# Hybrid decoder step: value product on four column groups of the array, and the normed input's split held resident and in HBM

## The chip, the cores and the metric

One core of one Trainium2 chip runs the whole step in one launch. The metric is the time of an execution on the device, in microseconds (us), lower is better. Engines are named as the profile names them: PE is TensorE (PEld its weight loads), DVE is VectorE, ACT is ScalarE, POOL is GpSimd, SP is SyncE, which here only issues DMAs.

## The reference

One layer for one prompt of 2048 tokens and eight decode rows with 4096 cached tokens each, d_model 1024, all in f32. The two edits touch the combined projection and, for the decode rows, the product of softmax weights with the cached values.

```
h = rms_norm(x, norm_g)
z = h @ w_in              # (1024 x 4096): ret q,k,v,gate | diff q,k,v,gate
# 4 retention heads: chunks of 128 tokens with a carried state, rms norm, times silu(gate)
# 4 differential heads: two softmax maps of 64 dims, a = p0 - lam * p1, o = a @ v
# decode rows: the same, with keys and values gathered by page_table from cache_k, cache_v
y = x + concat(o_ret * silu(gate), o_diff * silu(gate)) @ w_out
```

A f32 product of z is made of three products of rounded parts (fp32r): high h with high w, high h with low w, low h with high w, where low = value - high.

## The kernel before

Five stages follow each other, each a block in which every engine runs its own program and semaphores order them.

Stage 1, `setup_stage` (to 123.7 us), norms 17 tiles (one of the decode rows, 16 of 128 prompt rows). For each n ACT squares x (L323), POOL makes the inverse root, DVE normalises (L380), PE turns the tile with eight transposes (L473) into two banks, and ACT and DVE each copy one half into the resident g.hT (`keep_a` L332, `keep_b` L390). Meanwhile PE projects the decode rows with w_in in eight column groups of 2 MB. SP issues, in its order, `load_w(n)` (L266, two buffers, waits for the product of group n-2), `load_x(2n+1)` and `load_x(2n+2)` (L261, three buffers), n from 1 to 7, then the eight chunks of the first head's weights (L306), which ACT and DVE split (L350, L457).

Stage 2, `retention_stage`, runs four heads in a loop; stage 3, `diff_stage`, four more. A head begins with its projection: for each of 16 tiles, PE does 24 matmuls (`project_tile`, L563 to L565) on the halves h_hi and h_lo, which ACT (`split_h_high`, L541) and DVE (`split_h_low`, L549) make from g.hT again in each head, three slots ahead. ACT takes the result out of the bank (`keep_z`, L581 on); rotation and gate follow on DVE and POOL, and in stage 3 also a norm of queries and keys: DVE's sums of squares, POOL's inverse root, DVE's scaling (L1368) and rotary steps, and the parts of the keys (L1380).

Beside each head one decode row is worked. During the projection its 16 pairs of key pages come through a ring of four slots; DVE multiplies each with the query (L620) and sums (L626). After a softmax over the pages (`row_softmax_dve`, `row_softmax_pe`, `row_softmax_act`), 16 pairs of value pages come through the same ring, and PE multiplies each page (128 tokens x 512) with its scores (128 x 8) into s.row_bank (`row_values`, L691), a pair as two matmuls on 8 of the 128 columns of the array. Each f32 matmul stands as two records in the trace. The pairs are placed among PE's other work by `pairs_at`: in stage 2, one pair in each of the chunks t=3 to 12 and two in t=13 to 15; in stage 3, one in each of the attention units i=2 to 15, and two in 6 and 7.

A chunk of stage 2 is, on PE: turn of the next query and key (L1031, L1032), values, inner product (L1038), outputs (L1058, L1059) and the state's increment (L1061); ACT and DVE copy and mask between these, and in t=5 to 12 also split the next head's weights (L523, L529). The stages 4 and 5 (the decode rows' end and the output projection) do not use what is changed.

Of the kernel before, what the change touches and what calls it, by code (L numbers as in the profile page):

```python
# [21 lines left out]
F32 = mybir.dt.float32  # L22
# [24 lines left out]


# [5 lines left out]
def shape_constants():  # L54
# [29 lines left out]
    own_head = np.zeros((HC, NH, P), f)  # L84
    for i in range(HC):
        own_head[i, i // 2] = 1.0
    pick_map = np.zeros((HC, P), f)
    for i in range(HC):
        pick_map[i, i % 2] = 1.0
    own_row = np.zeros((NS, NS, P), f)  # L90
    for i in range(NS):
# [8 lines left out]
        "c_own_head": own_head.reshape(HC, NH * P),  # L100
# [90 lines left out]
def setup_stage(nc, io, g):  # L191
    with ExitStack() as ctx:
        sb = lambda n, s, d=F32: ctx.enter_context(nc.sbuf_tensor(n, s, d))
        sem = lambda n: ctx.enter_context(nc.semaphore(n))
# [15 lines left out]
        hsT = sb("hsT", [P, DC, NS])  # L210
        zs = sb("z_sample", [NS, 4 * D])
# [20 lines left out]
        kept_b = sem("s1_kept_b")  # L232
        z_ready = sem("s1_z_ready")
# [23 lines left out]
        def _(sp):  # L257
# [57 lines left out]
            sp.wait_ge(stored, 48)  # L315

        @block.scalar
        def _(act):
# [7 lines left out]
            def keep_a(n):  # L326
                act.wait_ge(turned, n + 1)
                src_ = bank[n % 2][:].rearrange("p (c r) -> p c r", c=4)
                if n == 0:
                    nc.scalar.copy(hsT[:, 0:4, :], src_[:, :, 0:NS]).then_inc(kept_a, 1)  # L330
                else:
                    nc.scalar.copy(g.hT[:, 0:4, (n - 1) * P:n * P], src_).then_inc(kept_a, 1)  # L332
# [38 lines left out]
        def _(dve):  # L371
# [12 lines left out]
            def keep_b(n):  # L384
                dve.wait_ge(turned, n + 1)
                src_ = bank[2 + n % 2][:].rearrange("p (c r) -> p c r", c=4)
                if n == 0:
                    dve.tensor_copy(hsT[:, 4:8, :], src_[:, :, 0:NS]).then_inc(kept_b, 1)
                else:
                    dve.tensor_copy(g.hT[:, 4:8, (n - 1) * P:n * P], src_).then_inc(kept_b, 1)  # L390
# [71 lines left out]
        def _(pe):  # L462
# [16 lines left out]
            pe.wait_ge(kept_b, 1)  # L479
            for n in range(8):  # L480
# [8 lines left out]
                turn(2 * n + 2)  # L489

# [17 lines left out]
HALVES = 2 * NT  # L508

# [22 lines left out]
def half_of_h(g, n):  # L532
    t, half = n // 2, n % 2
    return g.hT[:, 4 * half:4 * half + 4, t * P:(t + 1) * P]


def split_h_high(act, s, g, it, n):

    if n >= s.HSLOTS:
        act.wait_ge(s.half_used, it * HALVES + n - s.HSLOTS + 1)  # L540
    act.copy(s.h_hi[n % s.HSLOTS][:], half_of_h(g, n)).then_inc(s.half_high, 1)  # L541


def split_h_low(dve, s, g, it, n):

    dve.wait_ge(s.half_high, it * HALVES + n + 1)
    if n >= s.HSLOTS:
        dve.wait_ge(s.half_used, it * HALVES + n - s.HSLOTS + 1)
    dve.tensor_tensor(s.h_lo[n % s.HSLOTS][:], half_of_h(g, n), s.h_hi[n % s.HSLOTS][:],  # L549
                      ALU.subtract).then_inc(s.half_low, 1)  # L550


def project_tile(pe, s, g, it, t):
# [3 lines left out]
    for half in range(2):  # L557
        n = 2 * t + half
        pe.wait_ge(s.half_low, it * HALVES + n + 1)
        hi, lo = s.h_hi[n % s.HSLOTS], s.h_lo[n % s.HSLOTS]  # L560
        for c in range(4):
            wc = 4 * half + c
            pe.matmul(s.z_bank[t % 2][:], hi[:, c, :], g.w_hi[:, wc, :], start=(wc == 0), stop=False)  # L563
            pe.matmul(s.z_bank[t % 2][:], hi[:, c, :], g.w_lo[:, wc, :], start=False, stop=False)  # L564
            last = pe.matmul(s.z_bank[t % 2][:], lo[:, c, :], g.w_hi[:, wc, :], start=False, stop=(wc == DC - 1))  # L565
        last.then_inc(s.half_used, 1)


def keep_z(act, s, g, it, t):
# [9 lines left out]
    act.wait_ge(s.half_used, it * HALVES + 2 * t + 2)  # L579
# [55 lines left out]
def row_softmax_dve(dve, s, g, it, step):  # L635
    sc = s.scores[:].rearrange("p g s -> p s g")
# [9 lines left out]
    elif step == 2:  # L646
        dve.wait_ge(s.row_pe, q + 2)
        dve.tensor_tensor(s.scores[:], s.scores[:], bc(s.row_bank[:, 0:HC].unsqueeze(1), [P, NPAGE, HC]),
# [7 lines left out]
    elif step == 5:  # L656
        dve.wait_ge(s.values_used, it * NPAIR + NPAIR + VALUES_CREDIT)
        dve.tensor_tensor(s.row_own[:], s.row_bank[0:HC, :], g.own_head[:], ALU.mult).then_inc(s.row_dve, 1)
# [5 lines left out]
def row_softmax_pe(pe, s, g, it, step):  # L664
# [10 lines left out]
    elif step == 3:  # L675
        pe.wait_ge(s.row_dve, d + 7)
        pe.matmul(s.row_bank[:], g.pick_map[:], s.row_own[:], start=True, stop=True).then_inc(s.row_pe, 1)


def row_softmax_act(act, s, it):  # L680
    act.wait_ge(s.row_dve, it * ROW_DVE + 4)
    act.activation(s.scores[:], s.scores[:], ACT.Exp, scale=QSCALE).then_inc(s.row_exp, 1)


def row_values(pe, s, it, j):

    if j == 0:
        pe.wait_ge(s.row_dve, it * ROW_DVE + 6)
    pe.wait_ge(s.ring_loaded[(NPAIR + j) % RING], ring_at(it, NPAIR + j))
    for i in range(2):  # L690
        last = pe.matmul(s.row_bank[0:HC, :], s.scores[:, 2 * j + i, :], s.ring[(NPAIR + j) % RING][:, i, :],  # L691
                         start=(j == 0 and i == 0), stop=(j == NPAIR - 1 and i == 1))
    last.then_inc(s.values_used, 1)
# [55 lines left out]
def shared_tensors(nc, ctx, s):  # L749
# [7 lines left out]
    s.scores = sb("scores", [P, NPAGE, HC])  # L757
# [3 lines left out]
    s.row_own = sb("row_own", [HC, 512])  # L761
# [11 lines left out]
    s.half_high = sem("half_high")  # L773
# [1242 lines left out]
```

## Time and profile before

| | |
|---|---|
| median of 3 runs | 2217.17 us (2214.16 to 2220.43) |
| profiled execution | 2217.28 us, span 2215.6 us |
| mean granted TensorE clock | 0.914 |
| stage 1, to the first projection matmul | 123.7 us |
| stage 2, four heads | 123.7 to 778.0 us |
| stage 3, four heads | 778.0 us to the start of stage 4 |
| stage 5, output projection | 1943 to 2215.6 us |
| DMA over the span | 237.36 MB, mean 107 GB/s |

The profile is one execution. An engine's busy share is a mean over stages that have different limits, so it is read stage by stage. In a timeline row the first number is the start in us, the second the time, and what stands in brackets is how long the engine had been idle and what ended that.

### The profile page before, as it was taken

The page shows a single profiled execution, that of the slowest core. Times are in us where ns is not written, and L with a number is a line of the kernel's source. Part 1 is how long each engine was busy: PE and PEld are TensorE (multiplying, and loading weights), DVE is VectorE, ACT ScalarE, POOL GpSimd, SP SyncE. Part 2 cuts the span into 40 slices and gives each one's busy share as a digit, 9 for nine tenths or more (in the row PEclk, how much of TensorE's full clock was granted, in tenths as well). Part 3 has the DMA queues.
Part 4 walks back from the last instruction along what each step waited for, and adds up shares of the span by engine and source line. Part 5 has one row for each costly group of instructions (what it writes and reads, how often), then busy time and mean ns, then how long its engine had stood idle before and what let it go on. Part 6 is the DMA issues. An engine that isn't in the chain of part 4 may idle for free. (4 is left out here: it accounts for less than half of the span.)

```text
span 2215.6 us, 34308 instructions
## 1 busy us (share of the span) xinstructions
PE 1841.8 (83%) x8316; PEld 1261.9 (57%) x8316; DVE 1361.4 (61%) x2561; ACT 811.1 (37%) x2203; POOL 591.8 (27%) x1500
## 2 busy tenths in 40 slices
PE   6778998998998798589885898858989579657998
PEld 2267476476486376356763566634666446416887
DVE  2569468478477368577586675876757767462121
ACT  2333332332332233356343564435644346410000
POOL 4612322322422424121342112421214311240000
PEclk9989899998998899699996999979999789858999
DMA  7633533532622532321132311323212241053441
GB/s 288 230 120 97 175 106 100 173 104 90 195 91 89 158 110 77 104 97 59 52 94 90 102 63 45 96 81 115 63 36 91 60 150 44 11 155 129 136 141 69
DMA packets 164068, 237.36 MB, mean 107 GB/s; under 512 B 14963, under 2 KB 77060, under 8 KB 163732
## 3 DMA queue, kind: packets, MB, share of 16 engines
q1 hardware_dynamic: 157828, 218.22, 31.5%
q0 software_dynamic: 6048, 17.11, 2.1%
q8 instruction: 55, 0.90, 0.2%
q14 instruction: 137, 1.12, 0.2%
HBM read 207.00 MB, written 28.28 MB: 106 GB/s over the span
## 5 line engine op out<-in xcount | busy, mean ns | idle before, releaser
L563 PE MATMUL s_z<-g_w_hi,s_h_hi 128*128 128x512 f32 x1024 | 416.8, 407 | 63.0 <-DVE s_h_lo L549 63.0
L564 PE MATMUL s_z<-g_w_lo,s_h_hi 128*128 128x512 f32 x1024 | 411.3, 402 | 0.0
L565 PE MATMUL s_z<-g_w_hi,s_h_lo 128*128 128x512 f32 x1024 | 410.7, 401 | 0.0
L541 ACT CAST s_h_hi<-g_hT 128x512 fp32r<-128x512 f32 x256 | 157.4, 621 | 480.0 <-PE s_z L565 455.1
L549 DVE TENSOR_TENSOR s_h_lo<-g_hT,s_h_hi 128x512 fp32r<-128x512 f32 x256 | 181.5, 714 | 150.1 <-ACT s_h_hi L541 114.7
L563 PEld LDWEIGHTS s_z<-g_w_hi,s_h_hi 128*128 128x128 f32 x1024 | 196.5, 192 | 123.6 <-DVE s_h_lo L549 77.8
L691 PE MATMUL s_row<-s_ring,s_scores 128*8 128x512 f32 x512 | 246.5, 610 | 1.4 <-DVE s_row_stat L655 1.3
L1290 ACT ACTIVATE s_weights<-s_sc,s_neg_max 128x512 f32<-128x512 f32 (+3 forms) x320 | 196.3, 625 | 75.3 <-DVE s_neg_max L1433 53.1
L565 PEld LDWEIGHTS s_z<-g_w_hi,s_h_lo 128*128 128x128 f32 x1024 | 196.4, 192 | 47.9
L564 PEld LDWEIGHTS s_z<-g_w_lo,s_h_hi 128*128 128x128 f32 x1024 | 196.9, 192 | 45.5
L1550 PE MATMUL s_o<-s_vg,s_aT 128*128 128x128 f32 x1088 | 152.0, 287 | 52.5 <-ACT s_aT L1272 48.9
L1428 DVE TENSOR_REDUCE s_chunk_min<-s_sc 128x1 f32<-128x512 f32 (+3 forms) x288 | 161.9, 616 | 49.7 <-PE s_sc L1537 49.5
L1550 PEld LDWEIGHTS s_o<-s_vg,s_aT 128*128 128x128 f32 x1088 | 130.9, 192 | 74.5 <-ACT s_aT L1272 73.4
L620 DVE TENSOR_TENSOR s_ring<-s_ring,s_q_row 128x1024 f32<-128x1024 f32 x128 | 159.4, 1246 | 1.9 <-DVE s_qk L962 0.6
L626 DVE TENSOR_REDUCE s_scores<-s_ring 128x16 f32<-128x1024 f32 x128 | 156.2, 1220 | 4.4
L733 POOL TENSOR_TENSOR s_fin_x<-s_o_ms,s_rsum 128x4 f32<-128x4 f32 x16 | 3.1, 194 | 522.2 <-DVE s_vg L719 522.2
L1536 PE MATMUL s_sc<-s_kT,s_qT 128*128 128x512 f32 (+3 forms) x320 | 134.9, 422 | 5.7 <-ACT s_kT L1240 3.0
L1537 PE MATMUL s_sc<-s_kT,s_qT 128*128 128x512 f32 (+3 forms) x320 | 117.6, 378 | 0.0
L1871 DVE TENSOR_TENSOR s_y<-s_y_bank,s_x_in 128x512 f32<-128x512 f32 (+1 forms) x34 | 21.9, 685 | 155.0 <-PE s_y_bank L1913 155.0
L1272 ACT COPY s_aT<-s_z 128x512 f32<-128x512 f32 (+3 forms) x160 | 81.6, 524 | 74.3 <-PE s_z L1522 72.9
L1452 DVE SCALAR_TENSOR_TENSOR s_weights<-s_weights,s_coef,s_weights 128x512 f32<-128x512 f32 (+3 forms) x160 | 101.8, 685 | 10.7 <-DVE s_coef L1445 10.7
L1911 PE MATMUL s_y_bank<-g_wo_hi,s_u_hi 128*128 128x512 f32 x272 | 108.0, 397 | 0.0
(228 smaller groups left out, 3062.1 us busy)
## 6 DMA issues: line engine op xcount, KB each, us to landing
s_ring<-in_cache_k SPq DMA_DIRECT2D x256, 256.0 KB, 2.7
s_ring<-in_cache_v SPq DMA_DIRECT2D x256, 256.0 KB, 2.8
w_raw<-in_w_in SPq DMA_DIRECT2D x8, 2048.0 KB, 8.4
s_w_raw<-in_w_in SPq DMA_DIRECT2D x64, 256.0 KB, 3.4
s_u_in<-u_scratch SPq DMA_DIRECT2D x17, 512.0 KB, 4.0
x_in<-in_x_prompt SPq DMA_DIRECT2D x16, 512.0 KB, 5.6
u_scratch<-s_u_out POOLq DMA_DIRECT2D x64, 128.0 KB, 2.5
s_x_in<-in_x_prompt SPq DMA_DIRECT2D x16, 512.0 KB, 4.0
```

Source lines behind the costliest of these rows:

```text
L541: act.copy(s.h_hi[n % s.HSLOTS][:], half_of_h(g, n)).then_inc(s.half_high, 1)
L549: dve.tensor_tensor(s.h_lo[n % s.HSLOTS][:], half_of_h(g, n), s.h_hi[n % s.HSLOTS][:], ALU.subtract).then_inc(s.half_low, 1)
L563: pe.matmul(s.z_bank[t % 2][:], hi[:, c, :], g.w_hi[:, wc, :], start=(wc == 0), stop=False)
L564: pe.matmul(s.z_bank[t % 2][:], hi[:, c, :], g.w_lo[:, wc, :], start=False, stop=False)
L565: last = pe.matmul(s.z_bank[t % 2][:], lo[:, c, :], g.w_hi[:, wc, :], start=False, stop=(wc == DC - 1))
L620: dve.tensor_tensor(slot[:], slot[:], bc(s.q_row[:].unsqueeze(1), [P, 2, 512]), ALU.mult).then_inc(s.keys_times_q, 1)
L626: dve.tensor_reduce(s.scores[:, 2 * j:2 * j + 2, :], s.ring[j % RING][:].rearrange("p i (s f) -> p i s f", f=DH), AX, ALU.add).then_inc(s. ...
L691: last = pe.matmul(s.row_bank[0:HC, :], s.scores[:, 2 * j + i, :], s.ring[(NPAIR + j) % RING][:, i, :], start=(j == 0 and i == 0), stop=(j ...
L1290: act.activation(dst, score_bank[e % 4][:, 0:w], ACT.Exp, bias=neg_max[i % 2][:, m:m + 1], scale=-1.0, accum_out=sums[i % 2][:, m, j:j + 1 ...
L1428: chain.step(dve.tensor_reduce(chunk_min[:, j:j + 1], score_bank[e % 4][:, 0:w], AX, ALU.min))
L1536: pe.matmul(b[:, 0:w], qT[i % 2][:, m, :], keys, start=True, stop=False)
L1550: last = pe.matmul(banks["o"][:, 0:P], aT[k % 2][:, x * P:(x + 1) * P], s.vg[:, kb, 0:P], start=(kb == 0), stop=(kb == i))
```

## The change

First, the split of the normed input is made once. In stage 1 ACT's `keep_a` copies both halves of a tile into the resident g.h_hi (rounded to fp32r; it takes the place of g.hT), and DVE's `keep_b` subtracts that from the bank into one of four buffers, from which SP stores it (`store_low`, two DMAs of 256 KB a tile) to a scratch in HBM. In the heads the two split functions are gone; PE takes the high part from g.h_hi, and SP reads the low part back in 32 DMAs of 256 KB per head through four slots (`load_low`), in its order ahead of key pages. The loop of page loads in SP is unrolled by tile for that. Stage 3's slots lie on memory that the attention uses, so SP waits for a new semaphore, weights_free, at a head's start. Stage 1's semaphores are cleared and a barrier follows, so that there are enough for what comes.

Second, `row_values` takes two pairs (a quad of pages) with four matmuls, each on its own group of 32 columns of the array and its own 32 partitions of row_bank, where they add up apart; the matmul that picks the heads (L677) sums them. The stationary operand is 32 columns wide: the 8 scores of the page and those of the next three, whose products are not used. The quads stand in stage 2 at chunks 4, 6, 8, 10 and 12 to 15, in stage 3 at units 3, 5, 7, 9, 11 and 13 to 15.

```diff
 def setup_stage(nc, io, g):
...
+            def store_low(t):
+                sp.wait_ge(kept_b, t + 2)
+                for half in range(2):
+                    sp.dma_start(io["h_low"][t, :, 512 * half:512 * half + 512],
+                                 low[2 * (t % 2) + half][:].rearrange("p c x -> p (c x)").bitcast(F32)).then_inc(low_stored[t % 2], 16)
+
             for n in range(1, 8):
                 load_w(n)
                 load_x(2 * n + 1)
                 load_x(2 * n + 2)
+                store_low(2 * n - 2)
+                store_low(2 * n - 1)
+            store_low(NT - 2)
+            store_low(NT - 1)
...
             def keep_a(n):
                 act.wait_ge(turned, n + 1)
...
+                for half in range(2):
+                    src_ = bank[2 * half + n % 2][:].rearrange("p (c r) -> p c r", c=4)
...
+                        last = nc.scalar.copy(g.h_hi[:, 4 * half:4 * half + 4, (n - 1) * P:n * P], src_)
+                last.then_inc(kept_a, 1)
...
             def keep_b(n):
-                dve.wait_ge(turned, n + 1)
...
+                dve.wait_ge(kept_a, n + 1)
...
+                t = n - 1
+                if t >= 2:
+                    dve.wait_ge(low_stored[t % 2], 32 * (t // 2))
+                for half in range(2):
...
+                    last = dve.tensor_tensor(low[2 * (t % 2) + half][:], src_,
+                                             g.h_hi[:, 4 * half:4 * half + 4, t * P:(t + 1) * P], ALU.subtract)
+                last.then_inc(kept_b, 1)
...
+    nc.clear_and_free_semaphores(used)
+    nc.all_engine_barrier()
...
+def load_low(sp, io, s, g, it, n):
+
+    k = it * HALVES + n
+    slot = n % LOWSLOTS
+    sp.wait_ge(g.low_used, k + 1)
     t, half = n // 2, n % 2
...
+    sp.dma_start(s.low[slot][:].rearrange("p c x -> p (c x)").bitcast(F32), io["h_low"][t, :, 512 * half:512 * half + 512]
+                 ).then_inc(g.low_loaded[slot], 16)
...
 def project_tile(pe, s, g, it, t):
...
-        pe.wait_ge(s.half_low, it * HALVES + n + 1)
-        hi, lo = s.h_hi[n % s.HSLOTS], s.h_lo[n % s.HSLOTS]
+        pe.wait_ge(g.low_loaded[n % LOWSLOTS], (s.first_head + it) * (16 * HALVES // LOWSLOTS) + 16 * (n // LOWSLOTS + 1))
         for c in range(4):
             wc = 4 * half + c
...
+            hi, lo = g.h_hi[:, wc, t * P:(t + 1) * P], s.low[n % LOWSLOTS][:, c, :]
...
+        last.then_inc(g.low_used, 1)
...
+def row_values(pe, s, it, jj):
+
+
+    if jj == 0:
         pe.wait_ge(s.row_dve, it * ROW_DVE + 6)
...
+    for j in (2 * jj, 2 * jj + 1):
+        pe.wait_ge(s.ring_loaded[(NPAIR + j) % RING], ring_at(it, NPAIR + j))
+    for q in range(COLS):
+        j, i = 2 * jj + q // 2, q % 2
+        last = pe.matmul(s.row_bank[QUAD * q:QUAD * (q + 1), :], s.scores_all[:, 2 * j + i:2 * j + i + QUAD // HC, :].rearrange("p g s -> p (g s)"),
+                         s.ring[(NPAIR + j) % RING][:, i, :], start=(jj == 0), stop=(jj == NPAIR // 2 - 1),
+                         tile_position=(0, QUAD * q))
+    last.then_inc(s.values_used, 2)
...
 def retention_stage(nc, io, g):
...
-        pairs_at = {t: ([t - 3] if t < 13 else [2 * t - 16, 2 * t - 15]) for t in range(3, NT)}
+        quads_at = {4: [0], 6: [1], 8: [2], 10: [3], 12: [4], 13: [5], 14: [6], 15: [7]}
...
+                for n in range(LOWSLOTS):
+                    load_low(sp, io, s, g, it, n)
                 load_sample_q(sp, io, s, it, it)
-                for j in range(NPAIR):
+                for j in range(RING):
                     load_pages(sp, io, s, g, it, it, j)
+                for t in range(NT):
+                    for n in (2 * t + LOWSLOTS, 2 * t + LOWSLOTS + 1):
+                        if n < HALVES:
+                            load_low(sp, io, s, g, it, n)
+                    if t + RING < NPAIR:
+                        load_pages(sp, io, s, g, it, it, t + RING)
...
 def diff_stage(nc, io, g):
...
+        quads_at = {3: [0], 5: [1], 7: [2], 9: [3], 11: [4], 13: [5], 14: [6], 15: [7]}
...
+                sp.wait_ge(weights_free, it + 1)
+                for n in range(LOWSLOTS):
+                    load_low(sp, io, s, g, it + NH, n)
...
+                act.sem_inc(weights_free, 1)
```

## Rows read from the trace of the kernel before

**Rows 1.** Section 1 of the page: busy us, share of the span, instructions of each engine.
```profile
PE 1841.8 (83%) x8316; PEld 1261.9 (57%) x8316; DVE 1361.4 (61%) x2561; ACT 811.1 (37%) x2203; POOL 591.8 (27%) x1500
```

**Rows 2.** Groups of instructions of the page (busy, mean ns; idle before, releaser).
```profile
...
L549 DVE TENSOR_TENSOR s_h_lo<-g_hT,s_h_hi 128x512 fp32r<-128x512 f32 x256 | 181.5, 714 | 150.1 <-ACT s_h_hi L541 114.7
...
L691 PE MATMUL s_row<-s_ring,s_scores 128*8 128x512 f32 x512 | 246.5, 610 | 1.4 <-DVE s_row_stat L655 1.3
```

**Rows 3.** Windows (us; busy and count of PE, PEld, DVE, ACT, POOL): two projections.
```profile
123.70:215.80 92.10, 92.10 (x384) 73.78 (x384) 75.10 (x95) 28.95 (x74) 19.44 (x21) 0.97 0.33 102
...
778.00:884.40 106.40, 97.02 (x404) 75.11 (x404) 78.34 (x126) 40.25 (x99) 36.09 (x96) 0.97 0.31 97
```

**Rows 4.** Timeline of stage 1 (start us, us, engine, line): DVE, ACT, SP.
```profile
34.47 1.28 DVE L380 SCALAR_TENSOR_TENSOR h_nat<-x_in,rstd,norm_g_rows 128x1024 f32<-128x1024 f32 x1 [8.47 <-POOLq L363]
...
70.67 1.05 ACT L323 ACTIVATE junk<-x_in 128x1024 f32<-128x1024 f32 x1
...
74.91 1.28 DVE L380 SCALAR_TENSOR_TENSOR h_nat<-x_in,rstd,norm_g_rows 128x1024 f32<-128x1024 f32 x1 [1.45 <-issue]
...
86.61 0.38 SPq L266 DMA_DIRECT2D w_raw<-in_w_in  x1
...
110.94 4.91 DVE L457 TENSOR_TENSOR g_w_lo<-w_raw,g_w_hi 128x512 fp32r<-128x512 f32 x8 [0.44 <-ACT g_w_hi L350]
```

**Rows 5.** DMA issues of the page: KB each, median us from issue to landing.
```profile
s_ring<-in_cache_k SPq DMA_DIRECT2D x256, 256.0 KB, 2.7
...
w_raw<-in_w_in SPq DMA_DIRECT2D x8, 2048.0 KB, 8.4
```

**Rows 6.** Timeline between a stage 2 projection and its chunks: DVE, PE.
```profile
377.31 1.50 DVE L620 TENSOR_TENSOR s_ring<-s_ring,s_q_row 128x1024 f32<-128x1024 f32 x1 [0.16 <-DVE s_qk L962]
...
382.60 0.47 PE L1031 MATMUL s_turn<-g_ident,s_qk 128*128 128x128 f32 x1 [6.67 <-DVEq L963]
```

**Rows 7.** Timeline of the chunks of stage 2, second head: PE and ACT.
```profile
390.27 0.42 PE L1031 MATMUL s_turn<-g_ident,s_qk 128*128 128x128 f32 x1
...
393.65 0.42 PE L1031 MATMUL s_turn<-g_ident,s_qk 128*128 128x128 f32 x1
...
403.63 0.28 ACT L712 ACTIVATE s_junk<-s_o 128x128 f32<-128x128 f32 x1 [2.01 <-PE s_o L1059]
...
403.89 0.61 ACT L523 CAST g_w_hi<-s_w_raw 128x512 fp32r<-128x512 f32 x1
...
403.96 1.88 PE L691 MATMUL s_row<-s_ring,s_scores 128*8 128x512 f32 x4
...
407.08 1.88 PE L691 MATMUL s_row<-s_ring,s_scores 128*8 128x512 f32 x4
...
435.26 3.60 PE L691 MATMUL s_row<-s_ring,s_scores 128*8 128x512 f32 x8
...
443.52 0.79 PE L563 MATMUL s_z<-g_w_hi,s_h_hi 128*128 128x512 f32 x1 [1.37 <-DVE s_h_lo L549]
```

**Rows 8.** Timeline of DVE in a stage 3 projection.
```profile
1130.04 0.42 DVE L1357 SCALAR_TENSOR_TENSOR s_vg<-s_th,s_vg 128x256 f32<-128x256 f32 x1
...
1137.17 0.69 DVE L1368 TENSOR_TENSOR s_zqk<-s_zqk,s_rq 128x512 f32<-128x512 f32 x1 [1.81 <-POOLq L1333]
...
1140.51 0.69 DVE L549 TENSOR_TENSOR s_h_lo<-g_hT,s_h_hi 128x512 fp32r<-128x512 f32 x1 [0.30 <-PE s_z L565]
...
1144.11 0.42 DVE L1357 SCALAR_TENSOR_TENSOR s_vg<-s_th,s_vg 128x256 f32<-128x256 f32 x1
```

**Rows 9.** Timeline at the start of a stage 3 head: PE.
```profile
1067.40 0.80 PE L563 MATMUL s_z<-g_w_hi,s_h_hi 128*128 128x512 f32 x1 [4.08 <-DVE s_h_lo L549]
```

**Rows 10.** Timeline of attention units of stage 3: PE (units 6, 7), DVE (late unit).
```profile
948.75 3.60 PE L691 MATMUL s_row<-s_ring,s_scores 128*8 128x512 f32 x8
...
958.51 3.60 PE L691 MATMUL s_row<-s_ring,s_scores 128*8 128x512 f32 x8
...
1038.62 2.48 DVE L1428 TENSOR_REDUCE s_chunk_min<-s_sc 128x1 f32<-128x512 f32 x4 [2.36 <-PE s_sc L1537]
```

More of the change, by code:

```diff
@@ L210, in setup_stage @@
         hsT = sb("hsT", [P, DC, NS])
+        low = [sb(f"low{i}", [P, 4, P], F32R) for i in range(4)]
         zs = sb("z_sample", [NS, 4 * D])
@@ L232, in setup_stage @@
         kept_b = sem("s1_kept_b")
+        low_stored = [sem(f"s1_low_stored{i}") for i in range(2)]
         z_ready = sem("s1_z_ready")
@@ L315, in _ @@
             sp.wait_ge(stored, 48)
+            for i in range(2):
+                sp.wait_ge(low_stored[i], 32 * (NT // 2))
         @block.scalar
@@ L676, in row_softmax_pe @@
         pe.wait_ge(s.row_dve, d + 7)
-        pe.matmul(s.row_bank[:], g.pick_map[:], s.row_own[:], start=True, stop=True).then_inc(s.row_pe, 1)
+        pe.matmul(s.row_bank[0:2, :], g.pick_map[:], s.row_own[:], start=True, stop=True).then_inc(s.row_pe, 1)
 def row_softmax_act(act, s, it):
     act.wait_ge(s.row_dve, it * ROW_DVE + 4)
-    act.activation(s.scores[:], s.scores[:], ACT.Exp, scale=QSCALE).then_inc(s.row_exp, 1)
-def row_values(pe, s, it, j):
-    if j == 0:
+    act.activation(s.scores, s.scores, ACT.Exp, scale=QSCALE).then_inc(s.row_exp, 1)
+def row_values(pe, s, it, jj):
+    if jj == 0:
         pe.wait_ge(s.row_dve, it * ROW_DVE + 6)
[L689 to L693, printed above, removed]
+    for j in (2 * jj, 2 * jj + 1):
+        pe.wait_ge(s.ring_loaded[(NPAIR + j) % RING], ring_at(it, NPAIR + j))
+    for q in range(COLS):
+        j, i = 2 * jj + q // 2, q % 2
[3 more added lines that the diff above has]
+    last.then_inc(s.values_used, 2)
 def row_store(pool, io, s, it, row):
@@ L1176, in diff_stage @@
         av_done = sem("av_done")
+        weights_free = sem("weights_free")
         block = ctx.enter_context(nc.Block())
-        pairs_at, left = {}, list(range(NPAIR))
-        for i in range(2, NT):
-            pairs_at[i] = [left.pop(0) for _ in range(2 if i in (6, 7) else 1)]
-        assert not left
+        quads_at = {3: [0], 5: [1], 7: [2], 9: [3], 11: [4], 13: [5], 14: [6], 15: [7]}
         NB = NT // 2
@@ L1971, in build @@
             hb = lambda n, sh, d=F32: heads.enter_context(nc.sbuf_tensor(f"g_{n}", sh, d))
-            g.hT = hb("hT", [P, DC, SEQ])
+            g.h_hi = hb("h_hi", [P, DC, SEQ], F32R)
+            g.low_loaded = [heads.enter_context(nc.semaphore(f"g_low_loaded{i}")) for i in range(LOWSLOTS)]
+            g.low_used = heads.enter_context(nc.semaphore("g_low_used"))
             g.w_hi = hb("w_hi", [P, DC, 512], F32R)
```

138 lines of the change are left out of this document (55 added, 83 removed).

## The prediction

> **What bounds the kernel now.** I read the busy table first: PE is busy 83% of the span, with no other engine near it [rows 1]. That share hides four kinds of stretch, so the windows come next. The reader is to see there that a stage 2 projection keeps PE busy all of its 92.1 us, with 384 matmuls, while a stage 3 projection takes 106.4 us of which PE is busy 97.0 and DVE 78.3 [rows 3]. So PE ends the first and something else paces the second. The groups tell what the two edits touch: the low split L549 is 181.5 us of DVE, with an idle time of which 114.7 us ended by ACT's high split, and the value product L691 is 246.5 us of PE [rows 2]. The timelines then say, stage by stage, what arrives last. Stage 1 is a chain of weight loads, squares, norms and copies [rows 4, 5]. In a chunk of stage 2 that has one value pair, PE follows itself from value to value, 3.12 us apart (403.96 to 407.08) [rows 7]. Between projection and chunks PE waits 6.67 us for DVE's rotation [rows 6]. In a stage 3 projection DVE repeats every 14.07 us (1130.04 to 1144.11) [rows 8]. Stages 4 and 5 are not touched.
>
> **Stage 1 gets longer.** The split itself is cheap: per tile ACT copies two halves instead of one, and DVE subtracts two instead of copying one. What costs is the place of the stores. SP issues in order, so load_w(n+1) now stands behind store_low(2n-1), which waits for keep_b(2n), which DVE runs after normalise(2n+1), whose x was queued behind load_w(n). Before, x was the only thing that held SP, and weight loads ran ahead. The new cycle: the 2 MB load lands in 8.4 us [rows 5]; x, a quarter of that size, 2.1 behind it (estimate); square to normalise 4.24 (70.67 to 74.91) [rows 4]; normalise 1.28; two subtracts at the 0.714 us of L549 [rows 2], 1.43; two issues at 0.38 [rows 4], 0.76. Sum 18.2 us. The first cycle is read directly, since its normalise began at 34.47: 34.47 + 1.28 + 1.43 + 0.76 = 37.9 for the second weight group, and five cycles more make 128.9 for the last, which was issued at 86.61 [rows 4]: +42.3. Its tail was 110.94 + 4.91 - 86.61 = 29.2 [rows 4]. Now it is a cycle of 18.2, the last tile's 4.24 + 1.43, and only then the first head's weights, which used to be fetched earlier: issue 0.38, landing 2.7 by the 256 KB row [rows 5], a cast of 0.6, the eight splits 4.91: 32.5, +3.3. Clearing the semaphores and the second barrier is in no row; it lies between nothing and the 7.8 us that pass between the end of the splits at 115.85 and the first matmul of stage 2 at 123.70 [rows 3], and I take 3. Together **+49**; 38 if x lands beside its weights (five times 2.1 less), 60 if the stores slow each cycle by 2. SP, ACT, DVE and PE all wait in this cycle, so nothing covers it.
>
> **Stage 2.** The projections stay: PE had no wait in them [rows 3], so taking 32 splits a head from ACT and DVE frees nothing there. The 32 low loads a head, 256 KB each, land in some 2.7 us [rows 5] and are prefetched four deep; two loads a tile against 5.75 us (92.1 / 16). I cost them at nothing; without that cover each tile would pay up to 2.7 us. Then the tail. DVE did the last keys after the last tile, a product of 1.50 us at 377.31 and then a sum, and PE's wait of 6.67 us ended behind them [rows 6]. Without 32 splits it does them before that tile is ready; the rotation starts some 2.7 us earlier and POOL's sine products, which ran beside the keys, become the last: I estimate 3 us saved (bounds 1.5 and 4.2), **-12** over four heads. The next head's first matmul waited 1.37 us for a split (443.52) [rows 7]; its low part is already there: **-4**.
>
> The value product: four records (two matmuls) take 1.88 us, eight take 3.60 [rows 7], so one record costs 0.43. A quad has eight. No row shows two of them sharing the array, so the price is bounded by 8 x 0.43 = 3.44 (no overlap) and 2 x 0.43 = 0.86 (all four groups together). The two records of a matmul use the same column group and the order of issue is kept, so only the second record of one and the first of the next can run together: five steps of eight, **2.15 us**. I take that, since it is the middle and follows from the order of the records. A chunk with a quad then costs PE 3.12 - 1.71 + 2.15 = 3.56 less what overlaps at its ends, some 3.3; a chunk without one can't fall to PE's 1.4, for it then goes with ACT: square 0.28 at 403.63, weight cast 0.61 at 403.89, turned copy, inner, mask [rows 7], about 2.4. The chunks from t=3 on, now from 393.65 to 435.26 + 3.60 + 0.9 = 439.8 [rows 7], 46.1 us, become 3.4 (t=3, still at half clock, as 390.27 to 393.65 [rows 7]) + 4.6 + 4 x 2.4 + 7 x 3.25 = 40.3. The clock is the open point: it is low in the chunks without values until the first value product comes (the chunk before is 3.38 us long), and four such chunks now stand between the quads. If they ran at that length again it would be +4. I take the middle, -4 a head, **-16**.
>
> **Stage 3.** Of the four splits in each DVE cycle of 14.07 us, two lie inside the wait for POOL's norm that ends at 1137.17 (1.81 us of it left) and two outside, 0.9 and 0.6 us (from 1140.51, and before 1144.11) [rows 8]. Without them the cycle is 12.5, still over PE's 11.5 (48 matmuls at 92.1 / 384 [rows 3]). Seven cycles give -11.3, the three splits ahead of the first tile another 2.1 and their waits 0.9: -14.3 a head, **-57**. Bound: 11 if page loads, which now stand before low loads in SP's order, hold a tile back. At the head's start PE waited 4.08 us to 1067.40 [rows 9]; low loads go when ACT leaves its last unit, 2.7 to landing [rows 5]: -2 for three heads, **-6**, and the change of stage gives nothing. The new wait for weights_free holds SP, and behind it the queries and pages, but no longer than that.
>
> In the attention units values are hidden as long as DVE and ACT pace: two units with two pairs each lie 9.76 us apart (948.75 to 958.51) [rows 10], as others with one do. Late units have DVE waiting 2.36 us for scores (1038.62) [rows 10], so there PE counts. Quads at 9, 11, 13, 14, 15 cost 2.15 - 1.71 = 0.44 more each, the pairs gone from 8, 10 and 12 give about 0.4 each: **+4**.
>
> Sum: 49 - 12 - 4 - 16 - 57 - 6 + 4 = -42. The profiled execution took 2217.28 us (median 2217.17, so no correction): **2175 us**.
>
> A page rule bears on the value product. The trace shows each further value record costing its full 0.43 us, four of them 1.88 and eight 3.60 [rows 7]. The Trainium skill, "TensorE: Matmul & The Clock Gate" (Part 3, Packing small matmuls), states that matmuls on other column groups run nearly together, 2.38 times as fast for three of them, in strict order. By 2.38 a quad would be 3.44 / 2.38 = 1.45 us, between my middle and the full overlap, and the time about 2150, nearest to A. "TensorEngine Tiling (Array Packing)" (Key Properties) states against the change that switching the tiling mode drains the engine; a switch stands before and after each quad here, and by that rule a quad gains less. No run here shows either.
>
> **The rivals.**
> A, full overlap: quads of about 0.95. Quad chunks fall to the 2.4 of ACT's chain; SP's page loads then limit the last four. Against the middle -4 a head in stage 2 and -4 in stage 3: 2175 - 16 - 17 = **2142**. For: the groups are independent. Against: two records per matmul in order.
> C, no overlap, ends slower: 3.44 a quad. In stage 2 a quad chunk takes 3.12 + 1.73 = 4.85, some 4.6 on the average with the last one shorter, and the chunks between cannot use the time they were given, being paced by ACT: 3.4 + 6 + 4 x 2.4 + 7 x 4.6 = 51.2, +5 a head and with the clock some +6.5, +26 instead of -16. In stage 3 1.73 more on five late units less hidden parts, +6 a head, +24 instead of +4. 2175 + 42 + 20 = **2237**. It decides from a quad of about 2.9 us on that stage 1 outweighs the rest.
> D, the stores do not lengthen stage 1, because loads already run far enough ahead: 2175 - 46 = **2129**. Against: the SP order is plain.
> E, the change does not do what it says in stage 3: low loads stuck behind page loads in SP's order, projections remain at 105: 2175 + 57 = **2232**. Against: DVE sums a page some two tiles before the low part behind it is needed.
>
> **How the numbers follow.** B (the forecast) 0.38, A 0.23, C 0.26, D 0.06, E 0.07. About 0.3%, 6.7 us, is what a measurement can tell from no change. B holds 2148 to 2205 by its bounds (-11 and +11 in stage 1, 3 a head of values either way). Faster: B 0.35, A 0.23, D 0.06 = 0.64; same: 0.03 of B, 0.03 of C and E = 0.06; slower 0.30. The range reaches to A and C with stage 1 at its bounds: **2128 to 2250**.
>
> **What would show it.** Stage 1: the SP rows of load_w spaced 18 us, and the first projection at about 172 instead of 123.70. Values: start to start of the quad's eight records, 0.43 (C), five steps (B), or nearly together (A), and the spacing of quad and plain chunks, with the granted clock beside them. Stage 2: PE's idle before L1031, 3.6 instead of 6.67. Stage 3: DVE's cycle 12.5, and no PE wait on a low load. It would be wrong first of all if the quad's records or the setup cycle have another length.

## The result, and the profile after

The changed kernel takes 2156.03 us (median of 4 runs, 2151.84 to 2158.10), the kernel before 2218.80 in the same sets of runs (2214.16 to 2226.56). The ratio is 0.9711, with a 95% interval of 0.9679 to 0.9744: faster by 2.9%, 62.8 us, where 42 were forecast. The profiled execution took 2157.04 us.

The busy table of the changed kernel, to set against [rows 1]: PE does as many instructions as before and is busy 115 us less.

```profile
span 2155.4 us, 33493 instructions
## 1 busy us (share of the span) xinstructions
PE 1726.8 (80%) x8316; PEld 1271.0 (59%) x8316; DVE 1200.6 (56%) x2322; ACT 675.1 (31%) x1964; POOL 568.3 (26%) x1500
```

To see where the time went, each trace is cut at the same events of PE: the first and last matmul of each projection, the first turn (stage 2) or first score (stage 3) behind it, the last state increment or the closing product of a head, and the next head's first matmul. The table gives the difference from the profiled execution of before, in us, summed over four heads. The experiments are told further down; they stand here so that they can be compared.

| kernel | stage 1 | st. 2 projection | wait to chunks | chunks | tails, starts | st. 3 projection | wait to units | units | starts, stage 4 | sum |
|---|---|---|---|---|---|---|---|---|---|---|
| changed | +51.3 | -3.7 | -9.2 | -12.8 | -1.7 | -43.1 | -20.2 | -18.7 | -1.6 | -60.2 |
| values only | +4.6 | -4.3 | +0.1 | -22.4 | -0.3 | -1.2 | +0.2 | -15.9 | -1.6 | -41.4 |
| low part only | +54.7 | -3.4 | -9.2 | -6.0 | -2.4 | -42.1 | -23.5 | +9.6 | -0.4 | -22.6 |
| one group | +53.9 | -9.3 | -9.2 | +13.3 | -2.7 | -43.3 | -20.9 | +47.3 | -2.9 | +25.6 |
| weights ahead of stores | +25.5 | -7.2 | -9.2 | -10.4 | -1.0 | -45.3 | -20.0 | -18.4 | -0.3 | -86.3 |
| four raw buffers | +48.5 | -2.7 | -9.2 | -22.5 | -1.8 | -43.9 | -19.3 | -14.7 | +2.0 | -63.8 |
| unread matmuls, st. 2 | +49.7 | -3.0 | -9.0 | -34.0 | -1.9 | -46.8 | -19.7 | -16.7 | +2.7 | -78.7 |
| all three | +24.4 | -4.9 | -9.0 | -35.1 | -1.0 | -47.0 | -20.9 | -17.5 | -1.0 | -112.9 |

Stage 5, which stands in no column, differs by less than 1 us. Each row is one execution. Where the code of a column is the same, executions differ by up to 6 us in stage 1 (48.5 to 54.7) and up to 4 in the units (-14.7 to -18.7). So stage 1 cost 51 us, stage 3 gave 84, and stage 2 gave 27.

**Stage 1.** SP's timeline of the changed kernel: load_w is L269, load_x is L264, the stores are L305. A row joins the four stores of two tiles; the second pair waits, within the row, for the next tile's subtract.

```profile
92.03 0.45 SPq L269 DMA_DIRECT2D w_raw<-in_w_in  x1
92.52 1.23 SPq L264 DMA_DIRECT2D x_in<-in_x_prompt  x2
106.11 3.19 SPq L305 DMA_DIRECT2D h_low_scratch<-low  x4
109.34 0.46 SPq L269 DMA_DIRECT2D w_raw<-in_w_in  x1
...
123.32 3.19 SPq L305 DMA_DIRECT2D h_low_scratch<-low  x4
126.56 0.44 SPq L269 DMA_DIRECT2D w_raw<-in_w_in  x1
```

The reader is to see that each weight load follows its stores at once and that nothing is issued between 93.75 and 106.11: SP stands at the wait in store_low. The cycle is 17.3 us (92.03 to 109.34), where it was 18.2 in the forecast, and the last weights are issued at 126.56; before, they ran ahead, the last at 86.61 [rows 4].

**The value product.** PE's timeline in chunks of the second head, to set against [rows 7]:

```profile
443.64 1.07 PE L709 MATMUL s_row<-s_ring,s_scores 128*32 128x512 f32 x8
444.64 0.49 PE L1055 MATMUL s_inner<-s_qkT 128*128 128x128 f32 x2
...
466.90 1.41 PE L709 MATMUL s_row<-s_ring,s_scores 128*32 128x512 f32 x8 [2.80 <-DMA s_ring<-in_cache_v]
...
476.90 1.17 PE L709 MATMUL s_row<-s_ring,s_scores 128*32 128x512 f32 x8 [2.72 <-DMA s_ring<-in_cache_v]
```

Eight records take 1.07 us (1.69 in the first quad, at 438.88, still at the lower clock), and the inner product behind them starts 1.00 us after the first of them; before, eight took 3.60 [rows 7]. The same quad seen through two narrow stretches of the timeline shows how: four records start together at 443.64 and end within 0.64 us, and the other four start together at 444.09.

```profile
443.64 0.64 PE L709 MATMUL s_row<-s_ring,s_scores 128*32 128x512 f32 x4
...
444.09 0.61 PE L709 MATMUL s_row<-s_ring,s_scores 128*32 128x512 f32 x4
```

The four matmuls thus run side by side in both of their two passes. The last quads, however, wait for value pages: 2.80 us at 466.90, 2.72 us at 476.90, with "DMA s_ring<-in_cache_v" as what ended the wait.

**Clock.** Windows of the changed kernel (us, busy time and count of PE, PEld, DVE, ACT, POOL, then the granted clock, DMA share, GB/s): a stage 2 projection, the chunks of the second head, a stage 3 projection.

```profile
174.90:266.60 91.70, 91.67 (x384) 74.48 (x384) 55.21 (x67) 12.43 (x45) 23.50 (x21) 0.97 0.62 202
...
424.30:479.70 55.40, 40.76 (x229) 27.28 (x229) 23.89 (x77) 20.72 (x73) 18.71 (x57) 0.78 0.54 162
...
801.80:897.00 95.20, 93.18 (x407) 75.59 (x407) 63.32 (x99) 22.86 (x69) 33.97 (x111) 0.98 0.63 191
```

The chunks of the same head in the kernel before:

```profile
382.60:439.70 57.10, 55.77 (x229) 26.98 (x229) 25.61 (x77) 20.10 (x72) 18.93 (x57) 0.89 0.54 164
```

The same 229 PE instructions take 40.8 us of PE where they took 55.8, but the part is only 1.7 us shorter, and its mean granted clock fell from 0.89 to 0.78. The clock has two levels here, 1.2 and 2.4 GHz, and time at the lower one counts half in the mean. So that is 2 x 0.22 x 55.4 = 24 us at the lower level, after 2 x 0.11 x 57.1 = 12.6. Narrower windows of the changed kernel tell where:

```profile
424.30:438.90 14.60, 12.81 (x55) 10.23 (x55) 6.79 (x25) 5.13 (x19) 0.00 (x0) 0.50 0.00 0
...
454.20:457.40 3.20, 3.12 (x14) 2.30 (x18) 1.98 (x6) 1.76 (x7) 2.11 (x3) 0.52 0.84 276
...
466.90:471.00 4.10, 3.85 (x18) 2.26 (x18) 0.84 (x3) 0.58 (x3) 2.63 (x4) 0.58 0.86 260
```

Up to the first quad the whole stretch is at the lower level, as it was before up to the first pair (0.50 from 382.60 to 394.00). The new stretches stand behind waits of PE: 2.74 us for ACT's copy of a turned chunk, up to 454.28, and the waits for pages at 466.90 and 476.90. In the stage 3 projection PE is now busy 93.2 of 95.2 us (before: 97.0 of 106.4 us [rows 3]).

**The waits.** PE before the first turn of a stage 2 head, and DVE's cycle in a stage 3 projection (L1380 opens each two tiles, L1391 waits for POOL's norm), to set against [rows 6, 8]:

```profile
424.30 0.48 PE L1048 MATMUL s_turn<-g_ident,s_qk 128*128 128x128 f32 x1 [4.36 <-DVEq L984]
```

```profile
1121.56 0.42 DVE L1380 SCALAR_TENSOR_TENSOR s_vg<-s_th,s_vg 128x256 f32<-128x256 f32 x1
...
1133.59 0.41 DVE L1380 SCALAR_TENSOR_TENSOR s_vg<-s_th,s_vg 128x256 f32<-128x256 f32 x1
...
1140.01 0.69 DVE L1391 TENSOR_TENSOR s_zqk<-s_zqk,s_rq 128x512 f32<-128x512 f32 x1 [1.12 <-POOLq L1355]
...
1145.59 0.42 DVE L1380 SCALAR_TENSOR_TENSOR s_vg<-s_th,s_vg 128x256 f32<-128x256 f32 x1
```

PE waits 4.36 us instead of 6.67. DVE's cycle is 12.0 us (1121.56 to 1133.59 to 1145.59) instead of 14.07, with 1.12 us of waiting for POOL in it, and PE's own 48 matmuls are just as long, 93.2 / 8 = 11.7.

### The profile page after: what moved, and what is told of

Its sections match the earlier page's. It is cut to its first block and busy times, and to the rows that moved or that the text cites. A ratio compares the mean times of both kernels' runs of the same rounds, so it can differ in the third digit from the quotient of the medians.

```text
span 2155.4 us, 33493 instructions
## 1 busy us (share of the span) xinstructions
PE 1726.8 (80%) x8316; PEld 1271.0 (59%) x8316; DVE 1200.6 (56%) x2322; ACT 675.1 (31%) x1964; POOL 568.3 (26%) x1500
## 5 line engine op out<-in xcount | busy, mean ns | idle before, releaser
L578 PE MATMUL s_z<-g_w_hi,g_h_hi 128*128 128x512 f32 x1024 | 408.5, 399 | 62.8 <-DMA s_low<-h_low_scratch 50.6
L580 PE MATMUL s_z<-g_w_hi,s_low 128*128 128x512 f32 x1024 | 411.4, 402 | 0.0
L579 PE MATMUL s_z<-g_w_lo,g_h_hi 128*128 128x512 f32 x1024 | 410.8, 401 | 0.0
L578 PEld LDWEIGHTS s_z<-g_w_hi,g_h_hi 128*128 128x128 f32 x1024 | 199.7, 195 | 118.3 <-DMA s_low<-h_low_scratch 55.9
L596 ACT COPY s_zqk<-s_z 128x256 f32<-128x256 f32 x128 | 47.7, 373 | 655.1 <-PE s_z L580 655.1
L579 PEld LDWEIGHTS s_z<-g_w_lo,g_h_hi 128*128 128x128 f32 x1024 | 196.2, 192 | 43.8
L580 PEld LDWEIGHTS s_z<-g_w_hi,s_low 128*128 128x128 f32 x1024 | 195.7, 191 | 41.9
L1553 PEld LDWEIGHTS s_sc<-s_kT,s_qT 128*128 128x128 f32 x320 | 69.3, 216 | 69.2 <-ACT s_weights L1311 54.4
L1929 PE MATMUL s_y_bank<-g_wo_lo,s_u_hi 128*128 128x512 f32 x272 | 106.3, 391 | 0.0
L1930 PE MATMUL s_y_bank<-g_wo_hi,s_u_lo 128*128 128x512 f32 x272 | 106.2, 390 | 0.0
```

The costliest lines, as they stand in the source:

```text
L578: pe.matmul(s.z_bank[t % 2][:], hi, g.w_hi[:, wc, :], start=(wc == 0), stop=False)
L579: pe.matmul(s.z_bank[t % 2][:], hi, g.w_lo[:, wc, :], start=False, stop=False)
L580: last = pe.matmul(s.z_bank[t % 2][:], lo, g.w_hi[:, wc, :], start=False, stop=(wc == DC - 1))
L1553: pe.matmul(b[:, 0:w], qT[i % 2][:, m, :], keys, start=True, stop=False)
L1929: pe.matmul(b[:], u_hi[k][:, c, :], w_lo[:, c, w], start=False, stop=False)
L1930: last = pe.matmul(b[:], u_lo[k][:, c, :], w_hi[:, c, w], start=False, stop=(c == DC - 1))
```

## The experiments

**The value product alone.** The kernel before with row_values, its constants and its places from the change, and nothing else of it.

```diff
-        pairs_at = {t: ([t - 3] if t < 13 else [2 * t - 16, 2 * t - 15]) for t in range(3, NT)}
+        quads_at = {4: [0], 6: [1], 8: [2], 10: [3], 12: [4], 13: [5], 14: [6], 15: [7]}
...
+                         tile_position=(0, QUAD * q))
```

> The kernel before with the value product on four column groups alone; splits, stores and projection as before. Theory (the groups run together, and late attention units were waiting for PE): the chunk part of a stage 2 head falls by 3 to 4 us (before 57 to 58) and the attention part of a stage 3 head by 4 to 5 us (before 162), together about 30 us: 2187. Rival (the attention part fell in the changed kernel because DVE and ACT lost their splits, not because of the values): stage 3 attention stays at 162 and only some 13 us are gained: 2204.

Measured: 2174.93 us, ratio 0.9805 (0.9768 to 0.9841; one of the four runs took 2189.08). The units of stage 3 fell by 15.9 us (forecast 16 to 20), so that gain belongs to the values and the rival falls. The chunks gave 22.4 us, well over the 12 to 16 expected. The chunks of its second head:

```profile
382.10:435.00 52.90, 38.81 (x229) 25.34 (x229) 24.11 (x77) 20.48 (x73) 18.68 (x57) 0.82 0.57 177
```

Its clock there is 0.82, 2 x 0.18 x 52.9 = 19 us at the lower level, less than in the changed kernel.

**The low part alone.** The changed kernel with row_values and pairs_at of before.

```diff
-        quads_at = {4: [0], 6: [1], 8: [2], 10: [3], 12: [4], 13: [5], 14: [6], 15: [7]}
+        pairs_at = {t: ([t - 3] if t < 13 else [2 * t - 16, 2 * t - 15]) for t in range(3, NT)}
...
-                         tile_position=(0, QUAD * q))
```

> The changed kernel with the value pairs of before (8 columns, one after the other, in the old places). Theory: stage 1 ends 51 us later, the stage 3 projections with the gap behind them are 16 us shorter each, the stage 2 tails 2.3 us and starts and projections some 2 us: 51 - 64 - 15 = -28, so 2189, and with the values-only kernel it adds up to what the whole change gave (about -62). Rival (the two parts need each other, the low reads delaying the value pages or the freed PE time being used by the projection): the two gains differ from the whole by over 10 us.

Measured: 2189.11 us, ratio 0.9843 (0.9827 to 0.9860), as the theory had it. Stage 1 and the stage 3 projections repeat those of the changed kernel to some 3 us. Whether the parts add up is less clear. 0.9805 x 0.9843 is 0.9651, where the whole gave 0.9711, some 13 us less gain; but the three intervals leave some 11 us open there, and in the profiled executions of the table the parts come to -64.0 and the whole to -60.2. So the rival's bound of 10 is neither passed nor kept for sure. Below the totals the two do act on each other, in opposite ways: the chunks give 22.4 and 6.0 alone and 12.8 together, while the units give 15.9 and -9.6 alone and 18.7 together.

For the chunks the sums over the windows of the four heads tell how, first with the values alone, then in the changed kernel:

```profile
sum 207.50, PE 154.25 PEld 100.93 DVE 99.38 ACT 81.83 POOL 75.20; mean PE 38.56 PEld 25.23 DVE 24.84 ACT 20.46 POOL 18.80
...
sum 217.20, PE 161.79 PEld 106.48 DVE 97.20 ACT 82.66 POOL 74.64; mean PE 40.45 PEld 26.62 DVE 24.30 ACT 20.67 POOL 18.66
```

Of the 9.7 us between them PE's idle time makes only 2.2; for 7.5 us PE is busy longer with the same instructions, at a lower clock (0.75, 0.82, 0.86 and 0.83 in the four heads with the values alone, 0.82, 0.78, 0.75 and 0.78 in the changed kernel). So it is not that the low reads hold the value pages back. Why the clock is lower with the low part is not shown. The low part alone, second head:

```profile
429.70:485.10 55.40, 53.61 (x229) 25.87 (x229) 25.35 (x77) 20.02 (x73) 18.52 (x57) 0.94 0.53 163
```

With the pairs, PE is busy 53.6 of 55.4 us and the clock is 0.94 (7 us at the lower level). With quads and the low part, 40.8 us and 0.78. Its units are 9.6 us longer than before although their values are those of before. The second head's, before and with the low part alone:

```profile
1187.90:1350.70 162.80, 133.92 (x734) 87.05 (x734) 107.08 (x262) 89.19 (x259) 22.86 (x78) 0.93 0.28 87
...
1189.80:1356.30 166.50, 138.03 (x734) 89.39 (x734) 107.88 (x261) 88.96 (x259) 23.15 (x79) 0.90 0.24 73
```

PE is busy 4.1 us longer with the same 734 instructions, at a clock of 0.90 instead of 0.93, and that is as much as the units grew. What lowers the clock there stays open.

**One column group.** The changed kernel with the four matmuls of a quad on the first group, one after the other.

```diff
-        last = pe.matmul(s.row_bank[QUAD * q:QUAD * (q + 1), :],
+        last = pe.matmul(s.row_bank[0:QUAD, :],
...
-                         tile_position=(0, QUAD * q))
+                         tile_position=(0, 0))
```

> The changed kernel, but the four matmuls of a quad all on the first group of 32 columns, adding up in one place; all else the same, instruction for instruction, except that the closing product uses one group. Theory (the groups are what saves time): eight records 0.43 us apart, 3.4 us a quad instead of 1.06; stage 2 and 3 give back some 10 us a head where page loads do not hide it, 2156 + 60 to 85 = 2216 to 2240. Rival (the 32-column operand or the fewer places save it): records as close as in the changed kernel and 2156.

Measured: 2242.81 us, ratio 1.0095 (1.0078 to 1.0111): slower than before, by 1%. PE's timeline:

```profile
441.58 3.62 PE L709 MATMUL s_row<-s_ring,s_scores 128*32 128x512 f32 x8
...
448.28 3.62 PE L709 MATMUL s_row<-s_ring,s_scores 128*32 128x512 f32 x8
```

The same eight records, with the same 32 columns, take 3.62 us instead of 1.07. So the groups are what saves time, not the width or the places. It is also the price of rival C, measured: had the groups not run together, the change would have lost 21 us (C's price was 20, 2237 after 2217).

**Weights ahead of the stores.**

```diff
+            load_w(1)
             for n in range(1, 8):
-                load_w(n)
                 load_x(2 * n + 1)
                 load_x(2 * n + 2)
+                if n < 7:
+                    load_w(n + 1)
                 store_low(2 * n - 2)
                 store_low(2 * n - 1)
```

> The changed kernel with one line of the first stage moved: the next weight group is issued ahead of the two stores that it stood behind. Theory (stage 1 grew because the weight load waited in SP's order behind stores that wait for the end of the chain): the cycle falls from 17.6 to some 11 to 12 us, stage 1 by about 35 us: 2121. Rival (stage 1 grew because of the added work or bytes, two copies, two subtracts and stores): the same cycle within 1 us, 2150 to 2156.

Measured: 2126.20 us, ratio 0.9558 (0.9542 to 0.9575). SP's timeline:

```profile
60.79 3.19 SPq L305 DMA_DIRECT2D h_low_scratch<-low  x4
64.02 0.94 SPq L264 DMA_DIRECT2D x_in<-in_x_prompt  x2
65.01 0.46 SPq L269 DMA_DIRECT2D w_raw<-in_w_in  x1
73.00 3.18 SPq L305 DMA_DIRECT2D h_low_scratch<-low  x4
...
78.32 0.38 SPq L269 DMA_DIRECT2D w_raw<-in_w_in  x1
...
95.62 0.38 SPq L269 DMA_DIRECT2D w_raw<-in_w_in  x1
```

Weights (L269) now come right behind the two x, 13.3 us apart in the rows (65.01 to 78.32; the last 17.3 behind that), and stores follow 12.2 us apart (60.79 to 73.00). Stage 1 is 25.8 us shorter in the table, so half of its growth was the order and not the work; 35 had been expected, with a shorter cycle than it came.

**Four raw weight buffers in stage 2.**

```diff
+    s.RAW = 4 if s.first_head == 0 else 2
...
-                    if 3 <= j < 3 + DC:
-                        load_weight_chunk(sp, io, s, it, j - 3, next_block)
+                    if 1 <= j < 1 + DC:
+                        load_weight_chunk(sp, io, s, it, j - 1, next_block)
```

> The changed kernel with four buffers instead of two for the raw weight chunks of stage 2, and their loads two places earlier in SP's order. Theory (the last quads wait for pages that stand in SP's order behind weight chunks, which wait for earlier splits): PE's waits for pages before the quads of t=13 to 15 (2.8, 1.3 and 2.7 us in the second head) and the wait of 2.7 us at t=9 for a late weight chunk go, the chunk part of a head falls from 54.3 to some 50 us: 2156 - 16 = 2140. Rival (the clock, at its lower level for 24 of these 54 us, or the page loads themselves set the chunks): within 1 us a head, 2152 to 2160.

Measured: 2150.48 us, ratio 0.9682 (0.9663 to 0.9700), which overlaps the interval of the changed kernel: in the total undecided. In the trace the chunks are 9.7 us shorter over four heads, by between 0.1 us (first head) and 6.8 us (second), not 16. The second head:

```profile
419.60:468.20 48.60, 36.56 (x229) 24.24 (x229) 25.09 (x77) 20.02 (x72) 19.10 (x57) 0.86 0.54 173
```

Its clock is 0.86, against 0.78, and PE is busy 36.6 us, against 40.8. But PE's waits for value pages, which the theory wanted gone, are still there: 7.1 us in this head, after 6.8. What fell are the waits for ACT's copies of turned chunks, 3.5 us after 6.9. Over the four heads PE is idle 1.7 us less in the chunks and busy 8.1 us less. So the step with the pages fails, and most of what was gained came through the clock.

**Unread matmuls in stage 2.** The changed kernel with matmuls whose results go nowhere, in PE's waits.

```diff
+                def fill(n):
+                    for _ in range(n):
+                        pe.matmul(s.z_bank[0][:], g.h_hi[:, 0, 0:P], g.h_hi[:, 0, 0:512], start=True, stop=True)
+
+                pe.wait_ge(s.z_kept, it * NT + NT - 1)
+                fill(16)
                 pe.wait_ge(s.z_post, it * (NT // 2) + NT // 2)
...
+                    if t in (0, 1, 2, 3, 5, 7, 9, 11):
+                        fill(2)
```

> The changed kernel with matmuls added in stage 2 whose results nobody reads: 16 in the wait of 4.4 us between projection and chunks, and two in each of the chunks t=0 to 3, 5, 7, 9 and 11, which have no quad. Theory (the quads took PE work away and the clock went to its lower level: 24 of the 54 us of a head's chunk part, 12.5 before; what was freed was partly given back so): time at the lower level in the chunk part under 10 us, chunk part 54.3 to some 49, 2156 - 20 = 2136. Rival (ACT's chain and page loads set the chunks at either clock): chunk part unchanged or longer by the added matmuls, 2156 to 2164.

Measured: 2137.17 us, ratio 0.9626 (0.9610 to 0.9643), as the theory had it: 19 us less than the changed kernel, for 128 matmuls more. PE's timeline at the start of a head's chunks, and the window of these chunks:

```profile
409.53 3.79 PE L1045 MATMUL s_z<-g_h_hi 128*128 128x512 f32 x16
414.10 0.33 PE L1054 MATMUL s_turn<-g_ident,s_qk 128*128 128x128 f32 x1 [0.78 <-DVEq L984]
...
415.46 0.71 PE L1045 MATMUL s_z<-g_h_hi 128*128 128x512 f32 x2
```

```profile
414.10:462.60 48.50, 38.91 (x245) 24.71 (x245) 24.45 (x77) 20.37 (x73) 18.52 (x57) 0.89 0.58 184
```

The 16 matmuls end 0.78 us before the turn, which starts no later than without them and now takes 0.33 us, not the 0.48 of the row at 424.30 above. The mean clock is 0.89 (2 x 0.11 x 48.5 = 11 us at the lower level), and the chunks are 34.0 us shorter than before over four heads. That is about the -32 of rival A. The rival of this experiment, that ACT's chain and the pages alone set the chunks, falls.

**All three together**, with 24 unread matmuls before the last key turn of stage 3 as well:

> The changed kernel with the weight group issued ahead of the stores in stage 1, four raw weight buffers in stage 2, the unread matmuls in stage 2, and 24 more of them in each stage 3 head between projection and the last key turn, where PE waits 6.8 us. Theory: -30 for the order, -16 for the buffers, -20 for the clock in stage 2, and 2 us a head in stage 3 (the first units at full clock), less 5 because buffers and clock overlap: 2156 - 79 + 5 = 2082. Rival (the three hide each other, pages being last in any case): the order alone, 2126.

Measured: 2099.58 us, ratio 0.9457 (0.9441 to 0.9472), 18 us short of the 2082 (the terms as they stand add up to 74 and not to 79, which makes 2087). The rival's 2126 falls too. The chunks, -35.1, hardly gain over the unread matmuls alone: in the second head the waits for ACT's copies fell from 4.2 to 1.0 us, and those for value pages rose from 4.1 to 6.8. The 24 matmuls in stage 3 did nothing that can be seen: its projection, wait and units are those of the kernel with unread matmuls in stage 2 alone, to some 1 us, and the clock in the units is 0.86 (the first of the rows below).

**Unread matmuls in the units of stage 3.** They go to the turn bank that comes next.

```diff
                     if i == 1:
+                        fill_next(10)
                         turn_keys(NB - 1)
...
+                    if i == 2:
+                        fill_next(10)
+                    if i in (4, 6, 8):
+                        fill_next(4)
```

> The kernel with all three edits, and unread matmuls in the first attention units of stage 3 as well: ten in each of the waits of 3.9 and 3.6 us in units 1 and 2, four in units 4, 6 and 8. Theory (the units up to 8 are paced by DVE and ACT, so the lower clock, 42 us of the 158 of a head there, costs little): the time at the lower level falls by half, the unit part by 2 us a head at most, 2092 to 2100. Rival (the lower clock cost stage 3 as much as it did stage 2): the unit part falls by 5 us a head or more, 2080.

Measured: 2096.32 us, ratio 0.9430 (0.9413 to 0.9447), against 2099.58. Windows of the second head's units, without these matmuls and with them:

```profile
1122.20:1281.10 158.90, 125.40 (x734) 88.40 (x734) 108.11 (x262) 89.57 (x259) 22.50 (x77) 0.86 0.24 76
```

```profile
1116.00:1273.20 157.20, 128.13 (x766) 90.85 (x766) 108.18 (x261) 90.00 (x259) 22.74 (x77) 0.94 0.25 77
```

The clock rises from 0.86 to 0.94, the lower level from 44 to 19 us, and the units are 1.7 us shorter in this head (1.4 us a head on the mean of four, which is little more than executions of the same units differ by; the intervals of the two times overlap). The early units hardly care for PE's clock, as they should if DVE and ACT pace them: the theory holds, the rival's 5 us do not.

**The first head's weights ahead of the last stores.** All three edits, and this:

```diff
-            store_low(NT - 2)
-            store_low(NT - 1)
             first = io["w_in"][0].rearrange("(c p) (m x) -> c p m x", p=P, x=P)
...
+            store_low(NT - 2)
+            store_low(NT - 1)
```

> The kernel with all three edits, and the first head's weights loaded ahead of the last two stores of stage 1 instead of behind them. Theory (what is left of the growth of stage 1 is partly the tail, since these weights now wait for the last subtract): the first projection starts some 7 us earlier than the 148.1 us of that kernel, 2092. Rival (the stores or the semaphore clearing set the end): no change, 2100.

Measured: 2095.19 us, ratio 0.9420 (0.9400 to 0.9439). The first projection starts at 139.0 us instead of 148.1, 9 us earlier; the medians differ by 4 only, and the intervals barely part. Of the growth of stage 1, some 26 us were the order of weights and stores, about 9 the tail (one execution each), and 15 remain for the added work, the clearing and the barrier. The clearing and the barrier are little of that, as the rows of the next section show.

## Why the prediction was right, and where it was off

The time lies in the range, and on the forecast side; the likeliest case itself is 19 us too slow, by terms that were off in both directions.

- Stage 1, forecast +49, is +51. The mechanism and the cycle (17.3 for 18.2) are right: moving the loads ahead of the stores took half of the growth back. That the sum comes so near is luck in part, as three terms were off and largely cancel. The last weights went out at 126.56 instead of 128.9, 40.0 us later than before and not 42.3. The tail behind them grew by 10.5 us and not by 3.3: the forecast had the first cast wait for one of the first head's eight weight loads, and it waits for all eight, 9.8 us from 150.99 to 160.78 where the forecast had 3.1. And from the end of the splits to the first matmul it is 8.6 us after 7.8, so clearing, barrier and the first low load cost 0.8 and not 3.

```profile
150.99 5.85 SPq L319 DMA_DIRECT2D w_raw<-in_w_in  x8
...
160.78 4.26 ACT L367 CAST g_w_hi<-w_raw 128x512 fp32r<-128x512 f32 x8 [11.98 <-DMA w_raw<-in_w_in]
161.43 4.91 DVE L480 TENSOR_TENSOR g_w_lo<-w_raw,g_w_hi 128x512 fp32r<-128x512 f32 x8 [11.31 <-ACT g_w_hi L367]
...
174.93 0.79 PE L578 MATMUL s_z<-g_w_hi,g_h_hi 128*128 128x512 f32 x1 [27.24 <-DMA s_low<-h_low_scratch]
```

- The quad, forecast 2.15 us, is 1.07: rival A. The step that failed is "the two records of a matmul use the same column group and the order of issue is kept". The records do not stand one matmul after the other: the first passes of all four start together, and so do the second. The Trainium skill, "TensorE: Matmul & The Clock Gate" (Part 3, Packing small matmuls), has matmuls on other column groups run together, 2.38 times as fast for three. The trace agrees: for four it is 3.62 / 1.07 = 3.4 times. The Trainium skill, "TensorEngine Tiling (Array Packing)" (Key Properties), states that a change of the tiling mode drains the engine. Hardly any of that shows here, as the product behind the quad starts 0.55 us after its second set of records (444.09 to 444.64), where the sets themselves are 0.45 apart.
- The chunks, forecast -16 with quads twice as long, are -12.8. That the two are near is luck: the quads were half as long, and the clock took most of that back. With quads as short as this the sum of A said -32, and that is about what came (-34.0) once the mean clock was held at the 0.89 of before. The forecast named the clock as the open point and priced it at 2 of a possible 4 us a head. It was mis-sized: in the second head 24 us of 55 at the lower level instead of 12.6, and the unread matmuls won 21 us back over the four heads. A's own time, 2142, missed mainly for the same reason.
- The wait behind the stage 2 projection, forecast -12, is -9.2; the starts, forecast -4, are -1.4 a head within stage 2, and the change of stage takes 1.3 back.
- The stage 3 projections with the wait behind them, forecast -57, are -63. (Seven cycles of 14.07 less 12.5 are 11.0 us a head and not the 11.3 of the forecast, 1 us in all.) DVE's cycle is 12.0, not 12.5; with that DVE and PE, 11.7, are nearly level.
- The start of a stage 3 head, forecast -6, gave nothing. The rows of the second one:

```profile
1062.88 2.49 SPq L564 DMA_DIRECT2D s_low<-h_low_scratch  x4
...
1069.17 0.79 PE L578 MATMUL s_z<-g_w_hi,g_h_hi 128*128 128x512 f32 x1 [4.01 <-issue]
```

PE starts 4.01 us after the closing product, as before [rows 9], and the profile names nothing that it waited for. SP issued the first loads at 1062.88 and they take 3.6 us at the median:

```profile
s_low<-h_low_scratch SPq DMA_DIRECT2D x256, 256.0 KB, 3.6
```

So the first half tile was there at about 1066.5, some 2.7 us before PE. The step that failed is that the split was the last thing PE waited for there. What holds PE is not shown, and was not tried. The turn of the loop alone it is not: in stage 2, which loops over heads in the same way, PE goes from the closing product (480.98, 1.87 us) to the next head's first matmul at 482.78 without a wait.
- The units, forecast +4, are -18.7, of which the values alone give 15.9. The forecast had quads at 0.44 us more than a pair each in late units; at 1.07 they are 0.64 us less, and fewer. A's -12 or so was too small; that all late units gained, and not a slack of 0.4 us each, is argued from this sum and was not tried by itself.

Of the rivals, D and E fell (stage 1 did grow, and no wait for a low part holds the stage 3 projections for more than the 2 us that PE is idle in them), and C's price was met when the groups were taken away.

## What to carry to other kernels

Small products on different column groups of the array are worth placing together: four took 1.07 us here, and two on one group 1.88 before. But PE time that is freed where PE then waits can come back as a lower clock: here that took 21 us of 34 in stage 2's chunks, while in the attention units a higher clock won only some 1 us a head. So look at the granted clock of the stage, and not at PE's busy time alone, before counting it as gained. And a store put into an in-order queue of loads costs what the loads behind it then wait for: place it behind the loads of the next step.

## What had not been expected of the hardware

Four f32 matmuls on four column groups, of two records each, ran as two sets of four: starts within 0.03 us of each other in each set and 0.45 us between the sets (443.64 and 444.09), 1.07 us in all. And work without any use made a kernel faster: 32 unread matmuls a head, 16 of them 3.79 us long in a wait, took 19 us off the time, with the mean clock of the chunks at 0.89 instead of 0.78.
